# A two-layer decoder trunk: expert rows moved through DRAM tables by slot instead of selection matmuls

## What is computed

```python
logits = jnp.einsum('bsd,de->bse', h, w_router)
top_v, top_i = lax.top_k(logits, 2)
top_w = jax.nn.softmax(top_v, axis=-1)
gate = jnp.sum(jax.nn.one_hot(top_i, 8) * top_w[..., None], axis=-2)
for e in range(8):
    y = y + gate[..., e:e + 1] * ((silu(h @ w1[e]) * (h @ w3[e])) @ w2[e])
x = x + y
```

## Time and profile before

| | |
|---|---|
| median of 3 runs | 1592.75 us (1591.43 to 1595.17) |
| profiled execution | 1593.62 us, span 1591.8 us |
| PE busy | 1549.4 us, 97% |
| DVE, ACT busy | 1267.9 us (80%), 1052.8 us (66%) |
| POOL busy | 5.9 us, 12 instructions |
| DMA | 445.34 MB, mean 280 GB/s |
| DVE low part of a chunk (L1127) | 448 times, mean 1755 ns |
| ACT high part of a chunk (L450) | 448 times, mean 1492 ns |
| granted TensorE clock, mean | 0.989 |

### The profile page before, as it was taken

The page is one execution under the profiler, slowest core; times in us unless marked ns, Lnnn a source line. Parts: engine busy times, 40 slices in busy tenths (PEclk is TensorE's granted clock), DMA queues, the critical chain, the costliest instruction groups (busy, mean ns, idle before and its releaser), DMA issues.

```text
span 1591.8 us, 23204 instructions
## 1 busy us (share of the span) xinstructions
PE 1549.4 (97%) x7253; PEld 1271.5 (80%) x7253; DVE 1267.9 (80%) x1329; ACT 1052.8 (66%) x1159; POOL 5.9 (0%) x12
## 2 busy tenths in 40 slices
PE   7999999999999899999999999999999999999997
PEld 6888888788888778878878878877887887887885
DVE  5885655446976679789789789789889979978978
ACT  6565544336564467677687687687778768767766
POOL 0000000000000000000000000000000000000000
PEclk9999999999999789999999999999999999999999
DMA  9444565358543679799899999999989989989985
GB/s 331 159 159 133 185 198 167 107 191 282 167 160 109 233 228 302 255 369 371 288 375 370 312 354 367 338 329 371 374 296 370 370 297 367 369 293 372 372 305 193
DMA packets 361372, 445.34 MB, mean 280 GB/s; under 512 B 17728, under 2 KB 272744, under 8 KB 361336
## 3 DMA queue, kind: packets, MB, share of 16 engines
q1 hardware_dynamic: 360768, 442.73, 82.1%
q0 software_dynamic: 480, 2.13, 0.4%
q10 hardware_dynamic: 88, 0.02, 0.0%
HBM read 443.76 MB, written 1.05 MB: 279 GB/s over the span
## 4 chain that ended last, share of the span: by engine, by line
PE 83%; DMA 4%; issue 4%; DVE 4%; ACT 3%; SPq 1%; DVEq 0%; ACTq 0%
PE bank L748 25%; PE bank L750 25%; PE bank L749 25%; DMA w_raw<-in_moe_w 4%; PE bank L1036 2%; ACT w_hi L450 2%; PE bank L1062 2%; DVE w_lo L1127 1%; SPq L351 1%; DVE hT_lo L1517 1%; PE bank L830 1%; PE bank L774 1%; ACT hT_hi L739 0%; DMA x_residual<-in_x 0%; PE bank L814 0%
## 5 line engine op out<-in xcount | busy, mean ns | idle before, releaser
L1127 DVE TENSOR_TENSOR w_lo<-w_raw,w_hi 128x1024 fp32r<-128x1024 f32 (+1 forms) x448 | 780.9, 1755 | 113.9 <-ACT w_hi L450 113.1
L450 ACT ACTIVATE w_hi<-w_raw 128x1024 fp32r<-128x1024 f32 (+1 forms) x448 | 663.9, 1492 | 160.2 <-PE bank L750 145.2
L748 PE MATMUL bank<-w_hi,hT_hi 128*128 128x512 f32 (+1 forms) x1424 | 568.4, 399 | 6.6 <-DVE hT_lo L1517 2.5
L750 PE MATMUL bank<-w_hi,hT_lo 128*128 128x512 f32 (+1 forms) x1424 | 555.6, 390 | 0.0
L749 PE MATMUL bank<-w_lo,hT_hi 128*128 128x512 f32 (+1 forms) x1424 | 554.4, 389 | 0.0
L748 PEld LDWEIGHTS bank<-w_hi,hT_hi 128*128 128x128 f32 x1424 | 269.3, 189 | 63.6 <-issue 6.7
L750 PEld LDWEIGHTS bank<-w_hi,hT_lo 128*128 128x128 f32 x1424 | 269.0, 189 | 56.7
L749 PEld LDWEIGHTS bank<-w_lo,hT_hi 128*128 128x128 f32 x1424 | 269.9, 190 | 50.8
L1122 DVE TENSOR_TENSOR w_lo<-w_raw,w_hi 128x2048 fp32r<-128x2048 f32 (+2 forms) x100 | 201.5, 2019 | 96.8 <-ACT w_hi L444 96.0
L444 ACT ACTIVATE w_hi<-w_raw 128x2048 fp32r<-128x2048 f32 (+2 forms) x100 | 169.6, 1699 | 161.1 <-PE bank L750 159.7
L748 PE MATMUL bank<-w_hi,hiddenM_hi 128*128 128x512 f32 x448 | 178.8, 399 | 1.1
(11 more groups left out here) (230 smaller groups left out, 1022.2 us busy)
## 6 DMA issues: line engine op xcount, KB each, us to landing
w_raw<-in_moe_w SPq DMA_DIRECT2D x448, 512.0 KB, 8.0
w_raw<-in_moe_w SPq DMA_DIRECT2D x448, 256.0 KB, 4.9
w_raw<-in_w_in SPq DMA_DIRECT2D x64, 512.0 KB, 4.6
w_raw<-in_dense_w SPq DMA_DIRECT2D x44, 512.0 KB, 4.8
w_raw<-in_dense_w SPq DMA_DIRECT2D x44, 256.0 KB, 2.8
w_raw<-in_w_out SPq DMA_DIRECT2D x16, 512.0 KB, 4.6
w_raw<-in_w_pool_proj SPq DMA_DIRECT2D x8, 512.0 KB, 4.5
w_raw<-in_w_attn_proj SPq DMA_DIRECT2D x8, 512.0 KB, 4.1
```

The costliest lines, as they stand in the source:

```text
L450: act.activation(whi[:, m % SLOTS, 0:n], raw8[m % 8][:, 0:n], ACT.Copy).then_inc(s_hi, 1)
L748: pe.matmul(dst, ahi, bhi, start=start, stop=False)
L750: return pe.matmul(dst, alo, bhi, start=False, stop=stop)
L1127: dve.tensor_tensor(wlo[:, m % SLOTS, 0:n], raw8[m % 8][:, 0:n], whi[:, m % SLOTS, 0:n], ALU.subtract).then_inc(s_lo, 1)
```

## The change

Two tables in DRAM, `x_by_slot` and `y_by_slot`, have 12 x 128 rows of 1024 (a row for each slot of each job). In layer 0, 16 DMAs of 512 KB fill all of the first and the overflow jobs' rows of the second with x; SP issues one behind each of the 16 projection chunks. After routing, DVE computes for each token and each of its two choices the row, `rowu` = 128 * expert + slot, with a correction for overflow jobs. ACT writes the scaled x as `xn`, and GpSimd scatters it into the table with four indirect DMAs (`s_xsc`).

The first job's x is still gathered with `selR` matmuls, now with the tiles in the outer loop. The x of each later job is loaded by SP (`xg`, 512 KB) behind the loads of the first four down chunks, and PE only transposes it, 8 transposes. ACT copies y of a job to `ysb` and SP stores it to the table (`store_y`), behind the loads of the next job's first 8 chunks. The scatter matmuls, `selT`, `y_lo`, the later selections and the additions in the job go away. After the last job GpSimd gathers the y rows with four indirect DMAs, and DVE adds each with its gate in an operation of 1024 columns.

Around routing: the router's logits are made transposed, 24 matmuls with 8 rows out and 256 columns, copied by DVE and transposed back by two transposes; the norm's reciprocal chain on DVE comes after this copy; ACT loads the Sqrt table earlier; the second `x_rows_lo` comes behind the selection; and matmuls whose result isn't used (`keep_busy`, 4, 9, 3 and 6 of 512 columns) stand where PE waits. New tiles in the permanent area are sized to multiples of 64 bytes per partition. The diff's core:

```diff
@@ -180,15 +182,23 @@
+        late = ExitStack()
+        sb("late_raws", [P, 4, FULL], F32, late)
+        xg = sb("x_slot_rows", [P, D], F32, late)
+        ysb = sb("y_slot_rows", [P, D], F32, late)
+        y0 = sb("y_first_choice", [P, TT, D], F32, late)
+        sb("late_hidden", [P, D], F32, late)
+        xn = sb("x_scaled_rows", [P, TT, D], F32, late)
+        yg = [[y[:, t, :] for t in range(TT)] for y in (y0, xn)]
+        late.close()
+        xslot = nc.dram_tensor("x_by_slot", (NJ * P, D), F32).ap()
+        yslot = nc.dram_tensor("y_by_slot", (NJ * P, D), F32).ap()
...
@@ -314,9 +329,14 @@
                     c += 1
-                for col in ZCOL:
+                fill = [xslot[P * j:P * j + P, :] for j in range(NJ)] + [yslot[P * j:P * j + P, :] for j in range(E, NJ)]
+                for q, col in enumerate(ZCOL):
                     for h in range(2):
                         load(c, k_halves(c, w, 512 * h, col, 512))
+                        if l == 0:
+                            if c == 2:
+                                sp.wait_ge(s_x, 16)
+                            sp.dma_start(fill[2 * q + h], X[:, h, :]).then_inc(s_xz, 16)
                         c += 1
...
@@ -370,15 +390,24 @@
                 group(up_chunk, i, e, 24, 6)
+                sp.wait_ge(s_xsc, 2 * TT * 16)
+                sp.wait_ge(s_g, i * 2 + 2)
+                sp.dma_start(xg[:], xslot[bass.ds(i * P + P, P), :]).then_inc(s_xg, 16)
                 group(down_chunk, i, e, 28, 0)
...
+            def store_y(i):
+
+                sp.wait_ge(m_y, i * 2 + (LEAD + 2))
+                sp.dma_start(yslot[bass.ds(i * P, P), :], ysb[:]).then_inc(s_ys, 16)
+
             def next_job(i, e):
...
                     group(up_chunk, i, e, JOB_CHUNKS + 4 * g, g)
+                store_y(i)
...
@@ -405,8 +434,11 @@
                     sp.dma_start(raw8[k][:, 128 * j:128 * j + 128], A["moe_w2"][0, 0, 0:P, 0:P]).then_inc(s_ld[k], 16)
+            store_y(njobs - 1)
+            sp.wait_ge(s_ys, njobs * 16 + 16)
+            sp.nop().then_inc(s_go, 1)
             for t in range(TT):
-                sp.wait_ge(m_xa, njobs * 4 + (2 * t + 2))
+                sp.wait_ge(m_xa, 2 * t + 2)
                 sp.dma_start(out[0, t * P:t * P + P, :], X[:, t, :]).then_inc(s_out, 16)
...
@@ -420,10 +452,20 @@
                     pool.dma_start(wr[:], A["moe_router"][0].rearrange("(k p) e -> p k e", p=P)).then_inc(s_wrl, 16)
-            pool.wait_ge(s_rt, 1)
-            for z in (yhi, ylo, selT[:]):
-                ins = pool.memset(z.bitcast(F32), 0.0)
-            ins.then_inc(s_y0, 1)
+            pool.wait_ge(s_xz, (2 * NJ - E) * 16)
+            pool.wait_ge(s_row, 1)
+            for c in range(2):
+                for t in range(TT):
+                    if c == 0:
+                        pool.wait_ge(s_xn, t + 1)
+                    pool.indirect_dma_start(xslot, bass.IndirectOffsetOnAxis(rowu[:, c * TT + t:c * TT + t + 1], 0),
+                                            xn[:, t, :], None).then_inc(s_xsc, 16)
+            pool.wait_ge(s_go, 1)
+            for t in range(TT):
+                for c in range(2):
+                    pool.indirect_dma_start(yg[c][t], None, yslot,
+                                            bass.IndirectOffsetOnAxis(rowu[:, c * TT + t:c * TT + t + 1], 0)
+                                            ).then_inc(s_yg[c * TT + t], 16)
...
@@ -602,6 +644,8 @@
                     ahead(c + 25)
+                else:
+                    act.activation(sq0[:, 0:1], cst[:, C_ONE:C_ONE + 1], ACT.Sqrt)
                 hT_hi(3 * l + 2, 16 + 8 * l, (2, 3))
...
@@ -684,6 +727,10 @@
             gathered_hi(0)
+            for t in range(TT):
+                act.activation(xn[:, t, :], X[:, t, :], ACT.Copy, scale=st[:, 3, t:t + 1]).then_inc(s_xn, 1)
+            act.nop().then_inc(m_y, LEAD)
+            act.nop().then_inc(s_ys, 16)
             act.wait_ge(s_gd, 1)
...
@@ -711,8 +758,7 @@
                         if first and u == 1:
-                            act.wait_ge(s_st, i + 1)
-                            act.activation(selT[:], bank[1][:, 0:S], ACT.Copy).then_inc(s_sts, 1)
+                            act.wait_ge(s_xsc, 2 * TT * 16)
                         silu_m(b, u)
...
@@ -735,9 +781,9 @@
                 act.wait_ge(s_use, i * JOB_CHUNKS + (MOE0 + JOB_CHUNKS))
+                act.wait_ge(s_ys, i * 16 + 16)
                 for j in range(2):
-                    act.activation(yhi[:, 4 * j:4 * j + 4, :], bank[6 + j][:].rearrange("p (k n) -> p k n", n=P),
-                                   ACT.Copy).then_inc(m_yhi, 1)
+                    act.activation(ysb[:, 512 * j:512 * j + 512], bank[6 + j][:], ACT.Copy).then_inc(m_y, 1)
                 split_m(d0 + 27, FULL, j8)
...
@@ -1005,7 +1051,13 @@
                 down_d(k, (1,))
+            def keep_busy(n, b):
+
+                for _ in range(n):
+                    pe.matmul(bank[b][:], aThi[:, 0, 0:P], aThi[:, 0:2, :], start=True, stop=True)
+
             layer(1, LAYER1, first=lambda: x_T(2, 1))
+            keep_busy(4, 5)
             x_T(3, 1)
...
@@ -1013,10 +1065,14 @@
                 for k in (2 * j, 2 * j + 1):
-                    for t in range(TT):
-                        ins = three(bank[4 + t][:, 0:E], hThi[:, k, t * P:t * P + P], hTlo[:, k, t * P:t * P + P],
-                                    wrhi[:, k, :], wrlo[:, k, :], k == 0, k == KC - 1)
+                    ins = three(bank[4][0:E, 0:S], wrhi[:, k, :], wrlo[:, k, :], hThi[:, k, :], hTlo[:, k, :],
+                                k == 0, k == KC - 1)
             ins.then_inc(s_rt, 1)
+            pe.wait_ge(s_lt, 1)
+            for t in range(TT):
+                ins = pe.transpose(bank[5][:, t * E:t * E + E], lgT[:, t * P:t * P + P], cst[0:E, C_ID:C_ID + E])
+            ins.then_inc(s_rl, 1)
+            keep_busy(9, 0)
             pe.wait_ge(s_mk, 1)
...
@@ -1024,33 +1080,33 @@
             pe.matmul(bank[7][:, 0:E], ones, tmp8[:, 1, :], start=False, stop=True).then_inc(s_pos, 1)
+            keep_busy(3, 0)
...
-                pe.wait_ge(s_sel, i + 1)
+                if isinstance(i, int):
+                    pe.wait_ge(s_sel, 1)
+                    for t in range(TT):
+                        pe.wait_ge(s_xrl, t + 1)
+                        for j in range(2):
+                            for q in range(4):
+                                k = 4 * j + q
+                                for x in (xrhi, xrlo):
+                                    ins = pe.matmul(bank[2 + j][:, q * P:q * P + P], x[:, t, k * P:k * P + P],
+                                                    selR[:, t, :], start=(t == 0 and q == 0 and x is xrhi),
+                                                    stop=(t == TT - 1 and x is xrlo), skip_group_check=True)
+                            if t == TT - 1:
+                                ins.then_inc(s_g, 1)
+                    return
+                pe.wait_ge(s_xg, i * 16)
                 for j in range(2):
...
                         k = 4 * j + q
-                        for t in range(TT):
-                            for x in (xrhi, xrlo):
-                                ins = pe.matmul(bank[2 + j][:, q * P:q * P + P], x[:, t, k * P:k * P + P],
-                                                selR[:, t, :], start=(t == 0 and x is xrhi),
-                                                stop=(t == TT - 1 and x is xrlo))
+                        ins = pe.transpose(bank[2 + j][:, q * P:q * P + P], xg[:, k * P:k * P + P], ident)
                     ins.then_inc(s_g, 1)
-            def scatter(i):
-
-                pe.wait_ge(m_ylo, i * 2 + LEAD)
-                for t in range(TT):
-                    for nh in range(2):
-                        for y in (yhi, ylo):
-                            ins = pe.matmul(bank[4 * t + 2 + nh][:], selT[:, t * P:t * P + P],
-                                            y[:, 4 * nh:4 * nh + 4, :], start=(y is yhi), stop=(y is ylo))
-                        ins.then_inc(m_sc, 1)
-
-            pe.wait_ge(s_xrl, 2)
             gather(0)
-            pe.wait_ge(s_y0, 1)
+            keep_busy(6, 0)
             pe.wait_ge(s_tab, 1)
...
@@ -1069,24 +1125,16 @@
                         chunk(c, [bank[4 + u][:]], hehi, helo, 0, 512, True, False, i * jd + it, tiles=1)
-                        if first and u == 1:
-                            scatter(i)
                         if not (first and u == 0):
...
                             hiddenT_m(b - 1, 1 - u)
-                        if first and u == 1:
-                            for t in range(TT):
-                                ins = pe.matmul(bank[1][:, t * P:t * P + P], selR[:, t, :], identR[:],
-                                                start=True, stop=True)
-                            ins.then_inc(s_st, 1)
                         chunk(c + 1, [bank[4 + u][:]], hehi, helo, 4, 512, False, True, i * jd + it, tiles=1)
...
```

(55 more changed lines are left out.)

69 lines of the change are left out of this document (21 added, 48 removed).

## The result

The changed kernel takes 1603.66 us, median of 4 runs (1601.58 to 1604.88), against 1592.49 us (4 runs) of the kernel before on the same chip: ratio 1.0067, 95% interval 1.0055 to 1.008. It is slower by 11 us; I had forecast 1563, and the range ended at 1580.

The account below looks back on a forecast made before the run. The prediction took TensorE to bound the job, with a DMA reserve, and the job start as second place. Terms -21.4, -2.1, -1.9, -7.1, -2.6, +3.9, +1 sum to -30.2 from 1593.6, giving 1563; range 1553 to 1580.

Parts of the forecast that it names:

- DMA ceiling and added traffic: Expert jobs: 1.05 MB more per job at a 372 GB/s ceiling needs 120.6 us, under the new 124.2 us job.
- signs of being wrong: Observations that would refute the forecast: jobs staying above 126 us, or GpSimd's DMAs lasting over 5 us each.
- Rival (c): Expert jobs: smaller DMA reserve, mixed DRAM reads and writes, ceiling 358 GB/s; 125.4 us a job, total 1572; chance 0.11.
- Gather in the job: Each job's gather: 32 matmuls become 8 transposes, 2.7 us less per job, -21.4 over eight, no wait for slot rows.
- Scatter: Job start: removed matmuls' 1.86 us gains nothing in jobs 1 to 7, -1.9 in job 0; small matmuls -2.1 over eight.
- y store: Next job's up phase: storing y delays chunk 8 by 1.4 us, unseen by TensorE since split four chunks ahead; 0.
- Routing: Once, between layers and experts: first expert matmul at 553.8, -7.1; first 13 expert matmuls at full clock, -2.6.
- rival (a): Routing: full clock isn't kept; gather, positions and first matmuls stay slow, 7.2 us back, total 1570; chance 0.17.
- Indirect scatters: After routing: GpSimd's four indirect DMAs done by 562.5, before ScalarE's need at about 564.5; 0, bound 10 us.
- The end: After the last job: y store, indirect gathers and additions replace scatter, additions and store; +3.9, bounds +1 to +12.
- Rival (d): Job 0 and the end: indirect DMAs at 9 us each, 36 us per four, make it slower, 1611; chance 0.05.
- Layer 0: 16 table fills of 512 KB, the first two ahead of chunks that are waited for; +1, bounds 0 to 4.

Follow-up runs that it names:

- before_shift64: Kernel before with a 64-byte pad moving the upper four raw buffers off a multiple of 256 bytes, to 144192; 1616.10 us, ratio 1.0149.
- late256: Changed kernel with one tile widened so the upper four raw buffers start at a multiple of 256 bytes, 145408; 1580.04 us, ratio 0.9921.
- thin_traffic: Changed kernel with slot load and y store cut to 64 of 1024 columns, plus 8 more fills in layer 0; 1600.8 us, ratio 1.0057.
- late_store: all256 with first Silu and product ahead of the fifth chunk's split and low part, y store moved behind the next job's slot load; 1556.38 us, ratio 0.9772.
- before_all256: Kernel before with two pads putting all eight raw buffers at multiples of 256 bytes; 1582.73 us, ratio 0.9938.
- all256: Changed kernel with all eight raw buffers at multiples of 256 bytes; 1564.67 us, ratio 0.9835.

## Why the prediction was wrong, point by point

**DMA ceiling and added traffic: the step that failed.** "Demand becomes (43.8 + 1.05)/0.372 = 120.6 us, under the new job time": the rate was wrong, since 372 was a mean of 385 and 348 and the change moved four buffers to 348; and the comparison was wrong, since a job's demand was averaged over a stretch that is full and one that idles. At 348 the up part is bound by its loads: its part of the period (table) grows by 3.3 us from before to before_shift64 and by 3.2 from late256 to after, 22 over seven, of the 23.6 that placement costs. Of the signs of being wrong that I had named, both came: jobs above 126 us, and DMAs of GpSimd that last over 5. Rival (c) had a lower rate, but 358, as an average over the job, and a mixture of reads and writes for its cause; all three were off.

**Gather in the job**, -2.7: right. Eight transposes in 0.8 us, no wait for the slot rows:

```profile
895.48 1.04 PE L1105 MATMUL bank<-shape_constants,x_slot_rows 128*128 128x128 f32 x8
896.28 0.48 PE L794 MATMUL bank<-w_hi,hiddenM_hi 128*128 128x512 f32 x1
```

**Scatter**, 0 in jobs 1 to 7: the growth of the wait was right (1.9), its consequence was missed: the longer wait brings the clock down. Gather, small matmuls and wait together stand in the first part of the period, and there the sum was right: 2.7 + 0.26 forecast, 3.0 measured (55.8 to 52.8 at the old placement, 56.1 to 53.2 at the new). The clock costs 0.5 us a job at the old placement (72.7 on the mean, 72.2 in the jobs without a fall) and nothing that can be seen at the new one.

**y store**, 0: mis-sized. The second part of the period, where nothing was forecast, grows by 1.4 us a job at the new placement (74.5 to 75.9), close to the 0.524/0.348 = 1.5 that the store takes; with store and slot load cut it grows by 0.3 (thin_traffic, which doesn't separate the two). At the old placement it grows by 1.5, of which 0.5 is the clock; that the rest is the store wasn't tested there. Moving the store is worth 0.7 at full rate (late_store). The argument that the chunk behind it is split four chunks ahead fails where those four aren't in hand. Gather, scatter and store together bring 11.0 us over seven periods at the old placement (889.4 to 878.4), where I had 20.7.

**Routing**, -7.1 and -2.6: mis-sized, though the first expert matmul came at 554.07 for 553.8 forecast. That is luck: TensorE reached the router's transposes 1.9 us earlier than before (533.96 for the earlier trace rows's 535.89), which no term had, and late256, at the old placement, reaches them at 536.66. From these transposes to the first expert matmul it is 25.0 us before and 20.1 in after and in late256: 4.9 for 7.1. Logits and selection came as early as forecast or 0.6 earlier (selection 10.5 behind the transposes, 11.1 forecast), but the gather took 6.9 us and not 3.5, since the clock wasn't kept. So rival (a) came true in the gather, for 3.4 of its 7.2 us. The first expert matmuls did run 0.23 apart, but see the next point.

**Indirect scatters**, 0: too low, within the bound. On ScalarE and TensorE of after:

```profile
569.29 0.38 ACT L744 ACTIVATE hiddenM<-bank 128x256 f32<-128x256 f32 x1 [4.33 <-DMA x_by_slot<-x_scaled_rows,row_of_choice]
```

```profile
570.19 0.44 PE L1118 MATMUL bank<-shape_constants,hiddenM 128*128 128x128 f32 x2 [1.74 <-DVE hiddenM L1574]
...
576.72 0.44 PE L1118 MATMUL bank<-shape_constants,hiddenM 128*128 128x128 f32 x2 [0.61 <-DVE hiddenM L1574]
```

The rows are in place at 569.3 and not 562.5; TensorE waits 1.74 and then 0.61, about what the clock had gained. To the first gather the change brings 6.5 us (645.37 to 638.83, late256) where I had 10.9: 2.2 are missing in routing, and 2.4 from the first expert matmul on (84.5 to 82.1 for a forecast of 4.8), about the 2.35 of this wait.

**The end**, +3.9: measured 19.1 us from the first y copy (1582.33) to the end, against 12.3 before, so +6.8, inside the bounds. GpSimd's four gathers, and the first addition:

```profile
1586.53 2.07 POOL L466 DMA_INDIRECT y_first_choice<-y_by_slot,row_of_choice  x1 [1023.70 <-SPq L439]
1588.90 0.97 POOL L466 DMA_INDIRECT x_scaled_rows<-y_by_slot,row_of_choice  x1 [0.30 <-issue]
```

```profile
1591.92 1.28 DVE L1614 SCALAR_TENSOR_TENSOR x_residual<-y_first_choice,gate_probs,x_residual 128x1024 f32<-128x1024 f32 x1 [4.17 <-DMA y_first_choice<-y_by_slot,row_of_choice]
```

The rows come 5.4 us after the first issue and not 3.6, and the issues are 2.4, 1.3 and 1.3 us apart on GpSimd, near the 1.4 that I took from bandwidth. Rival (d) was false: one of the scatters took 9.3 us to land, but the four overlap, 14.6 us from the first issue to the last landing and not 36.

**Layer 0**, +1: at like placement TensorE reaches the same row in layer 0 at 131.53 (before_all256) and 131.85 (all256), so 0.3. At the router's transposes the pairs of like placement differ by +0.4, +0.8 and -0.8, so an effect of this size can't be told there.

Together, against the forecast of 1563: 24 us from placement, 10 from the seven periods (by these parts mostly the y store, and some clock at the old placement), 4 up to the first gather, 3 at the end, 41 in all, and 40.7 measured. all256 came out at 1564.67, next to the forecast, but that doesn't bear it out: the kernel before gains 9.1 us from the same placement, and those weren't in the sum.

## What to carry over

Before a tile is added, work out where the DMA destinations behind it will lie; a buffer for 1 KB rows belongs at a multiple of 256 bytes, and 64 isn't enough. When a rate looks like a ceiling, look at it in slices as short as one transfer: two values in turn are two kinds of transfer, and the mean of them is no limit. A reserve of an engine counts only in the stretch that lacks it, and the same holds for a fall of TensorE's clock: it can follow a wait that grows "under cover", and it cost up to 0.9 us where TensorE was nearly the limit and nothing where loads were.
